# Leaving out the wait between the two passes of the inversion products

## The reference

```python
def wkv_scan(state0, r, w, k, v, kk, a, reverse):
    ...
    def step(S, inp):
        r_t, w_t, k_t, v_t, nkk_t, b_t = inp
        sa = jnp.einsum('bhvk,bhk->bhv', S, nkk_t)
        S = S * w_t[:, :, None, :] + sa[..., None] * b_t[:, :, None, :] + v_t[..., None] * k_t[:, :, None, :]
        return S, jnp.einsum('bhvk,bhk->bhv', S, r_t)
```

## Time and profile before

| | |
|---|---|
| median of 3 runs | 4236.55 us |
| the profiled execution | 4238.25 us, of which the span 4236.6 us |
| PE busy | 3822.1 us, 90% |
| weight loads (PEld) | 3441.3 us, 81% |
| DVE busy | 2386.9 us, 56% |
| ACT busy | 1629.7 us, 38% |
| records of line 990 on PE, 5120 | from 2526.6 us to 3281.8 us |

### The profile page before, as it was taken

The page is one execution under the profiler, slowest core; times in us unless marked ns, Lnnn a source line. Parts: engine busy times, 40 slices in busy tenths (PEclk is TensorE's granted clock), DMA queues, the critical chain, the costliest instruction groups (busy, mean ns, idle before and its releaser), DMA issues.

```text
span 4236.6 us, 82998 instructions
## 1 busy us (share of the span) xinstructions
PE 3822.1 (90%) x33100; PEld 3441.3 (81%) x33100; DVE 2386.9 (56%) x4281; ACT 1629.7 (38%) x2283; POOL 24.2 (1%) x47
## 2 busy tenths in 40 slices
PE   7999989989899999969996768888888889999998
PEld 6988877779899999957895446666666789999998
DVE  4769985664777774444353236656565444444443
ACT  4545542333454543331232232223221245555433
POOL 0000000000000000000000000000000000000000
PEclk9999999999999999989997868666667799999999
DMA  4546654344455555522243420000000345555553
GB/s 155 182 162 256 259 224 160 146 159 169 144 183 183 183 176 181 181 97 89 99 145 106 171 93 3 4 6 4 5 4 3 129 139 179 182 184 180 175 181 118
DMA packets 80704, 571.90 MB, mean 135 GB/s; under 512 B 9488, under 2 KB 9744, under 8 KB 15472
## 3 DMA queue, kind: packets, MB, share of 16 engines
q1 hardware_dynamic: 78048, 558.50, 37.1%
q0 software_dynamic: 2448, 10.46, 0.7%
HBM read 566.82 MB, written 2.10 MB: 134 GB/s over the span
## 4 chain that ended last, share of the span: by engine, by line
PE 78%; DVE 15%; issue 3%; ACT 2%; DMA 1%; DVEq 0%; POOL 0%; SPq 0%; ACTq 0%
PE po L254 16%; PE po L255 16%; PE po L256 16%; PE po L1427 6%; PE pa L990 3%; DVE w_lo L242 2%; PE po L990 2%; PE pa L300 1%; DVE s_v L680 1%; DMA raw<-ada 1%; PE pa L897 1%; PE po L468 1%; DVE hf L311 1%; PE pa L1726 1%; PE po L469 1%
## 5 line engine op out<-in xcount | busy, mean ns | idle before, releaser
L242 DVE TENSOR_TENSOR w_lo<-raw,w_hi 128x1024 fp32r<-128x1024 f32 x880 | 1040.2, 1201 | 466.0 <-ACT w_hi L235 450.0
L235 ACT ACTIVATE w_hi<-raw 128x1024 fp32r<-128x1024 f32 (+1 forms) x877 | 898.0, 1037 | 799.3 <-PE po L256 576.9
L254 PE MATMUL po<-hh,w_lo 128*128 128x256 f32 x3744 | 1062.9, 284 | 24.4 <-DVE hh L335 12.6
L255 PE MATMUL po<-hh,w_hi 128*128 128x256 f32 x3744 | 1061.3, 283 | 0.0
L256 PE MATMUL po<-hh,w_hi 128*128 128x256 f32 x3744 | 1061.2, 283 | 0.0
L254 PEld LDWEIGHTS po<-hh,w_lo 128*128 128x128 f32 x3744 | 720.7, 192 | 28.9 <-issue 28.6
L255 PEld LDWEIGHTS po<-hh,w_hi 128*128 128x128 f32 x3744 | 720.8, 193 | 0.0
L256 PEld LDWEIGHTS po<-hh,w_hi 128*128 128x128 f32 x3744 | 720.6, 192 | 0.0
L254 PE MATMUL po<-f_hi,w_lo 128*128 128x256 f32 x1408 | 400.1, 284 | 6.1 <-DVE f_lo L1609 6.1
L255 PE MATMUL po<-f_lo,w_hi 128*128 128x256 f32 x1408 | 399.8, 284 | 0.0
L256 PE MATMUL po<-f_hi,w_hi 128*128 128x256 f32 x1408 | 399.8, 284 | 0.0
(11 more groups left out here) (545 smaller groups left out, 6852.8 us busy)
## 6 DMA issues: line engine op xcount, KB each, us to landing
raw<-ffn_up SPq DMA_DIRECT2D x176, 1024.0 KB, 4.8
raw<-w_in SPq DMA_DIRECT2D x112, 1024.0 KB, 4.8
raw<-ada SPq DMA_DIRECT2D x96, 1024.0 KB, 5.6
raw<-ffn_down SPq DMA_DIRECT2D x64, 1024.0 KB, 4.9
raw<-w_out SPq DMA_DIRECT2D x32, 1024.0 KB, 4.8
raw<-ffn_down SPq DMA_DIRECT2D x32, 768.0 KB, 4.2
raw<-glu SPq DMA_DIRECT2D x16, 1024.0 KB, 5.6
raw<-dn_proj SPq DMA_DIRECT2D x8, 1024.0 KB, 5.3
```

The source lines that it names most:

```text
L235: act.activation(w_hi[:, k % 4, 0:width], raw[:, k // 2 % ring, (k % 2) * PW:(k % 2) * PW + width], ACT.Copy).then_inc(hi_ready, 1)
L242: dve.tensor_tensor(w_lo[:, k % 4, 0:width], raw[:, k // 2 % ring, (k % 2) * PW:(k % 2) * PW + width], w_hi[:, k % 4, 0:width].bitcast(F32 ...
L254: pe.matmul(po[bank][:, 0:T], lo, act_hi[:, t, :], start=first and n == 0, stop=False)
L255: pe.matmul(po[bank][:, 0:T], hi, act_lo[:, t, :], start=False, stop=False)
```

## The change

The second pass no longer waits until the last product of the first has signalled, and the semaphore increment of that product is gone. The call of `settle` stays before the first pass only. The products, their order, their banks and the signals at the end of the call are as before.

```diff
         def blocks_pe(pe, n, sets, k, outs, lhs, rhs):
 
             for swap in range(2):
-                if swap:
-                    pe.wait_ge(j_half, n * 10 + k)
-                settle(pe)
+                if not swap:
+                    settle(pe)
                 mm = [None, None]
...
                         mm[e] = pe.matmul(o, lhs[e][r, m, :], w, start=True, stop=True)
-                if swap == 0:
-                    mm[1].then_inc(j_half, 1)
             for e in range(2):
                 mm[e].then_inc(sets[e][0], 1)
```

## The result

The changed kernel takes 4168.77 us (median of 4 runs, 4164.69 to 4174.13), the kernel before 4237.51 us beside it. The ratio is 0.9835, with a 95% interval of [0.9813, 0.9858]: 69 us faster, 60 to 79 by the interval. The forecast was 40 us, and a range down to 4170 us. The direction was right, the size was not.

The account below looks back on a forecast made before the run. PE was taken as the busiest engine, 82% of the recurrence stage. 58 us of holes x 0.71 gave 41, less 1 for chunk waits, 40 us: 4197 us forecast (own range 4182 to 4208; with rivals 4170 to 4221).

Parts of the forecast that it names:

- The hole: Between the helper's two passes on PE: removing the wait saves 0.36 us a call, 58 us for 160 calls.
- The rival that the array holds the second pass back: Between the passes: the array delays the second until the first has left; 18 us saved, 4219 us, chance 0.12.
- The share on the path: DVE sat idle for the helper's output in 114 of 160 calls, so 71% of 58 us, 41 us, counts.
- What is late next: PE's waits for k_ur (38.6 us) and k_S (25.9 us) in the chunk stream may lengthen; 1 us charged.
- The clock: Granted PE clock of the recurrence stage, mean 0.69: left unchanged in the forecast, so no time counted for it.
- the 0.04 that the prediction had named as its own refutation: Sign: if the stage's mean granted clock moves by more than 0.04, the prediction's clock term was wrong.
- the clock rises: Rival in the recurrence stage: fuller stretches raise the clock, 40 + 30 us saved, 4167 us, chance 0.09.
- 8 points: Clock estimate for the stage: eight points of full-clock share either way are 61 us of stage, some 30 us of time.
- one fall of the clock behind a sparse stretch: Trace evidence after 2596 to 2604 us: clock falls from 1.00 to 0.79 behind sparse PE work, not dense work.

Follow-up runs that it names:

- e10: The changed kernel with every product of both passes made twice, no wait between them; 4234.0 us, ratio 0.9991 to the kernel before.
- e11: The kernel before, wait kept, with every product of both passes made twice; 4279.35 us, ratio 1.01 to the kernel before.
- e5: The changed kernel, no wait, with the first pass making the products of blocks 2 and 3 a second time; 4164.16 us, ratio 0.9821 to the kernel before.
- e9: The kernel before, wait kept, with the first pass making the products of blocks 2 and 3 a second time; 4239.46 us, ratio 0.9999.
- e8: The kernel before with a second wait of the same kind in the middle of each first pass, 320 waits for 160; 4325.5 us, ratio 1.0203.
- e2: The changed kernel with the increment of settled put back between the passes, without the wait; 4160.8 us, ratio 0.9826 to the kernel before.
- e3: The kernel before with the wait kept only in the 80 first calls of a level; 4174.9 us, ratio 0.9853.
- e4: The kernel before with the wait kept only in the 80 second calls of a level; 4194.1 us, ratio 0.9894.

## Why the prediction missed

- **The hole.** Taken at 0.36 us, 58 us for all calls; measured 0.36 and 0.29 in the two calls shown, and 55 us over all 160. The half step for the change of tiles is there (0.14 against a step of 0.107, 0.09 against 0.058). The rival that the array holds the second pass back wanted about 0.3 us between the passes and is out. The Trainium skill's rule on row tiles ("TensorEngine Tiling (Array Packing)", Gotcha 1) speaks of simultaneous access to one bank. Here the exchange of the two diagonal tiles puts the first product of the new pass behind the last one in the same tile, and the trace shows no price beyond that half step. Whether the two tiles ever touched one bank at the same moment no run shows, since the ends of matmuls are modelled.
- **The share on the path.** 71%, 41 us. With the clock nearly pinned (e10, e11) the 160 waits cost 45 us, of holes that add up to 53. With an interval of 34 to 58 us this agrees with the term, and does not fix the share closer than to two thirds or more.
- **What is late next.** The waits for k_ur and k_S did grow, from 67.6 to 94.2 us over the whole program, but they did not eat the gain: 1 us was charged. That their growth and the gain go together is shown; how much more would have been gained without it isn't.
- **The clock: the step that failed.** "I leave the clock where it is in the forecast." It rose from 0.69 to 0.77, twice the 0.04 that the prediction had named as its own refutation. So a term of 24 to 30 us stood in the sum as nothing. What the text missed is that the two terms are not independent: the direct 41 to 45 us make the stage shorter with the same products in it, and the clock rises with that (e5, e9, e10). The rival "the clock rises" gave 4167 us, 2 us from the result, with a chance of 0.09. The range, said to reach down to it, stopped at 4170, short of both. The rival had the right effect and no mechanism, and its nearness to the result is luck, of two errors that cancel: full-clock share went up by 16 points, not 8, and they brought 24 to 30 us, not 30 for 8 points. By the prediction's own steps 61 us at 0.107 us a step become 33 at 0.058, so 28 us with PE on the whole chain, and about 14 with PE on half of it. The argument drawn from the earlier trace rows, one fall of the clock behind a sparse stretch, was evidence for the mechanism, and it was used to call the matter balanced. The Trainium skill's "TensorE: Matmul & The Clock Gate" (section on the HAM clock gate: activity releases the throttle) was quoted in the prediction, and the runs agree: from e8 through the kernel before and e5 to e10, 0.62, 0.69, 0.84 and 0.90, more products made in the stage's time went with a higher clock. Neighbours can stand the other way round, as e9 (0.77 at 13.7 records a us) and e2 (0.82 at 13.4).

So the forecast had the chain right and lacked one factor: about 45 us direct became 69. What stays open is why the gain isn't additive over the calls (e3, e4): saturation of the clock and the chunk stream's chain both fit, and no run separates them.

## What to carry to other kernels

In a stage whose granted clock lies between its two levels, an edit's direct saving isn't its price: here 160 holes cost 45 us with the clock held high and 69 to 75 us with it free. Forecast such a stage with a feedback term, and measure it cheaply by repeating products that are already there: if work added on the path costs nothing and the granted clock goes up with it (e5, e9), the clock is paying. Either sign alone is not enough, since work off the path costs nothing too. And put a wait that an engine must make on itself where nobody else's input is behind it: between the passes it cost 69 to 75 us, at the end of the call 18 to 26.

## What was not expected of the hardware

- Repeated products were free: 1280 records more (14%) left the time at 4164 us against 4169 without the wait, and at 4239 against 4236 with it. That holds for this amount: 5120 more without the wait (e10) took the time to 4234 us.
- A wait of PE for its own last product opens a hole of 0.50 us between starts at 1.2 GHz and 0.38 at 2.4, while an increment in PE's queue in the same place opens none.
- Two executions of nearly the same program (changed, e2) had stage clocks of 0.77 and 0.82, and stages of 694 and 677 us, while the ratios of the two kernels to the one before agree (0.9835 and 0.9826).
